# Expert routing: 136 candidate sums per token, and the second expert tile of six heads as three rounded passes

## The reference, cut to what matters

```python
q = (hb @ w_pq).reshape(TOK_BLOCK, PEER_HEADS, 2, PEER_DHALF)
s = jnp.einsum('thpd,hpnd->thpn', q, sub_keys).astype(jnp.float32)
s1, i1 = lax.top_k(s[:, :, 0], PEER_TOPK)          # PEER_TOPK = 16, of 128 keys
s2, i2 = lax.top_k(s[:, :, 1], PEER_TOPK)
cand_s = (s1[..., :, None] + s2[..., None, :]).reshape(..., PEER_TOPK * PEER_TOPK)
top_s, pos = lax.top_k(cand_s, PEER_TOPK)
gate = jax.nn.softmax(top_s, axis=-1)
act = jax.nn.gelu(jnp.einsum('thkd,td->thk', expert_u[idx], hb), approximate=False)
```

## Time and profile before

| | us |
|---|---|
| time, median of 3 runs | 2181.74 |
| lowest and highest | 2181.66, 2182.7 |
| profiled execution, its own time | 2179.3 |
| its span | 2177.5 |

### The profile page before, as it was taken

The page is one execution under the profiler, slowest core; times in us unless marked ns, Lnnn a source line. Parts: engine busy times, 40 slices in busy tenths (PEclk is TensorE's granted clock), DMA queues, the critical chain, the costliest instruction groups (busy, mean ns, idle before and its releaser), DMA issues.

```text
span 2177.5 us, 42049 instructions
## 1 busy us (share of the span) xinstructions
PE 2141.2 (98%) x15321; PEld 1926.4 (88%) x15321; DVE 1460.8 (67%) x2770; ACT 1039.6 (48%) x1757; POOL 104.1 (5%) x78
## 2 busy tenths in 40 slices
PE   9999999999999999999999999999999999999999
PEld 7999998899899987899998668889889999999998
DVE  5556998655655547655685578989886666666665
ACT  4335776533533337433562455458534444444443
POOL 0000000000010000000000004600000000000000
PEclk9999999999999999999999999999999999999999
DMA  6555664455566544555541024344667666655553
GB/s 218 188 182 176 211 191 139 155 193 176 171 209 213 185 137 127 181 176 188 168 145 52 20 98 146 135 159 155 208 224 240 209 204 203 211 185 183 191 185 133
DMA packets 107725, 374.12 MB, mean 172 GB/s; under 512 B 11984, under 2 KB 17888, under 8 KB 107376
## 3 DMA queue, kind: packets, MB, share of 16 engines
q1 hardware_dynamic: 102848, 354.88, 48.8%
q0 software_dynamic: 4784, 18.00, 2.8%
HBM read 362.29 MB, written 13.69 MB: 173 GB/s over the span
## 4 chain that ended last, share of the span: by engine, by line
PE 90%; DVE 6%; ACT 1%; DVEq 1%; issue 1%; DMA 0%; POOL 0%; ACTq 0%
PE bank L357 72%; PE bank L386 5%; PE bank L1590 2%; PE bank L2653 2%; DVE w_lo L309 1%; PE bank L563 1%; PE bank L339 1%; PE bank L341 0%; DVE arena L2839 0%; DVE arena L2832 0%; ACT w_hi L304 0%; PE bank L581 0%; PE bank L2172 0%; DVE arena L2833 0%; PE bank L346 0%
## 5 line engine op out<-in xcount | busy, mean ns | idle before, releaser
L309 DVE TENSOR_TENSOR w_lo<-ring,w_hi 128x1024 fp32r<-128x1024 f32 x575 | 695.4, 1223 | 410.3 <-ACT w_hi L304 408.0
L304 ACT ACTIVATE w_hi<-ring 128x1024 fp32r<-128x1024 f32 x599 | 624.7, 1056 | 627.0 <-PE bank L357 562.8
L357 PE MATMUL bank<-u_hi,w_hi 128*128 128x256 f32 x2712 | 771.4, 284 | 6.6 <-POOL w_lo L309 4.7
L357 PE MATMUL bank<-u_hi,w_lo 128*128 128x256 f32 x2712 | 767.4, 283 | 0.0
L357 PE MATMUL bank<-u_lo,w_hi 128*128 128x256 f32 x2712 | 767.3, 283 | 0.0
L357 PEld LDWEIGHTS bank<-u_hi,w_hi 128*128 128x128 f32 x2712 | 519.7, 192 | 18.8 <-issue 7.4
L357 PEld LDWEIGHTS bank<-u_lo,w_hi 128*128 128x128 f32 x2712 | 519.7, 192 | 7.5 <-issue 0.5
L357 PEld LDWEIGHTS bank<-u_hi,w_lo 128*128 128x128 f32 x2712 | 519.7, 192 | 0.0
L357 PE MATMUL bank<-w_hi,x_hi 128*128 128x512 f32 x992 | 390.7, 394 | 1.3 <-DVE x_lo L2156 0.9
L357 PE MATMUL bank<-w_lo,x_hi 128*128 128x512 f32 x992 | 388.2, 391 | 0.0
L357 PE MATMUL bank<-w_hi,x_lo 128*128 128x512 f32 x992 | 386.1, 389 | 0.0
(11 more groups left out here) (316 smaller groups left out, 1816.9 us busy)
## 6 DMA issues: line engine op xcount, KB each, us to landing
ring<-in_w SPq DMA_DIRECT2D x264, 512.0 KB, 3.6
ring<-in_expert_u SPq DMA_DIRECT2D x128, 512.0 KB, 3.5
ring<-in_expert_v SPq DMA_DIRECT2D x128, 512.0 KB, 4.2
ring<-in_ssm_in SPq DMA_DIRECT2D x40, 512.0 KB, 4.5
gate_dram<-con SPq DMA_DIRECT2D x16, 576.0 KB, 2.8
arena<-gate_dram POOLq DMA_DIRECT2D x9, 1024.0 KB, 8.8
ring<-in_ssm_out SPq DMA_DIRECT2D x16, 512.0 KB, 4.0
ring<-in_w_o SPq DMA_DIRECT2D x16, 512.0 KB, 3.8
```

The lines of the kernel that those rows point to most:

```text
L304: act.activation(w_hi[slot][:, :], ring[slot][:, :], ACT.Copy).then_inc(hi_made[slot], 1)
L309: dve.tensor_tensor(w_lo[slot][:, :], ring[slot][:, :], w_hi[slot][:, :].bitcast(F32), ALU.subtract).then_inc(freed[slot], 1)
L357: mm = pe.matmul(out, left[a], right[b], start=start and n == 0, stop=stop and n == 2, skip_group_check=True)
```

## The change

The candidates become 136: the sums of row 0 with all 16 columns, and of rows 1 to 15 with columns 0 to 7. (A pair that has at least 16 better or equal pairs ahead of it can't be among the 16 best; with both lists in order, no pair of a row past the first with a column past the eighth can.) The row and the column of a pick come from its index by a shift and three small float operations. The second expert tile of heads 1 to 6 goes by `project_split`: ACT makes its `w_hi` at the end of `tiles`, and POOL its `w_lo` right behind that of the first tile. Those of heads 0 and 7 stay with `project`.

```diff
-    "pre_plain": (PH, [0, 0, 0, 1]),
+    "pre_plain": (1, [0, 0, 0, 1]),
+    "pre_second": (PH - 2, [0, 0, 0, 1]),
+    "pre_end": (1, [0, 0, 0, 1]),
...
-            def plain_tile(i):
-                arrived(pe, 3, "pre_plain", i)
+            def second_tile(i):
+                out = bank[(2 * i + 1) % 4][:, 0:T]
                 pe.wait_ge(S("pre_gelu"), 2 * i + 2)
-                project(pe, bank[(2 * i + 1) % 4][:, 0:T], 3).then_inc(freed[3], 1)
+                if 0 < i < PH - 1:
+                    project_split(pe, out, 3, "pre_second", i - 1)
+                else:
+                    arrived(pe, 3, "pre_end" if i else "pre_plain")
+                    project(pe, out, 3).then_inc(freed[3], 1)
...
                 pre(2 * i)
-                multiplied(act, 3, "pre_plain", i)
+                if 0 < i < PH - 1:
+                    split_done(act, 3, "pre_second", i - 1)
+                else:
+                    multiplied(act, 3, "pre_end" if i else "pre_plain")
                 pre(2 * i + 1)
+                if i < PH - 2:
+                    make_hi(act, 3, "pre_second", i)
...
                 if 0 < i < PH - 1:
                     make_lo(pool, 2, "pre_split", i)
+                    make_lo(pool, 3, "pre_second", i - 1)
                 if 0 < i < PH - 2:
                     pool.wait_ge(S("cands_made"), i + 1)
                     make_lo(pool, 0, "route_a", i - 1)
...
-                ins = dve.tensor_tensor(cand.rearrange("p t (a b) -> p t a b", a=TOPK), top[:, 0:TT, :].unsqueeze(3).broadcast_to([P, TT, TOPK, TOPK]),
-                                        top[:, TT:2 * TT, :].unsqueeze(2).broadcast_to([P, TT, TOPK, TOPK]), ALU.add)
+                dve.tensor_tensor(cand[:, :, 0:TOPK], top[:, TT:2 * TT, :],
+                                  top[:, 0:TT, 0:1].broadcast_to([P, TT, TOPK]), ALU.add)
+                ins = dve.tensor_tensor(cand[:, :, TOPK:NCAND].rearrange("p t (a b) -> p t a b", b=NEAR),
+                                        top[:, 0:TT, 1:TOPK].unsqueeze(3).broadcast_to([P, TT, TOPK - 1, NEAR]),
+                                        top[:, TT:2 * TT, 0:NEAR].unsqueeze(2).broadcast_to([P, TT, TOPK - 1, NEAR]), ALU.add)
...
-                dve.tensor_scalar(as_int(flat(best_a)), as_int(flat(best_i)), 4, None, ALU.logical_shift_right)
-                dve.tensor_scalar(as_int(flat(best_b)), as_int(flat(best_i)), 15, None, ALU.bitwise_and)
-                dve.drain()
-                dve.tensor_copy(best_abf, as_int(best_ab))
+                dve.tensor_scalar(as_int(flat(best_row)), as_int(flat(best_i)), 3, None, ALU.logical_shift_right)
+                dve.drain()
+                dve.tensor_copy(best_foundf, as_int(best_found))
+                dve.drain()
+                dve.scalar_tensor_tensor(flat(best_row), flat(best_rowf), 2.0, flat(best_rowf), ALU.is_ge, ALU.mult)
+                dve.tensor_scalar(flat(best_af), flat(best_rowf), 1.0, 0.0, ALU.subtract, ALU.max)
+                dve.drain()
+                dve.scalar_tensor_tensor(flat(best_bf), flat(best_row), -float(NEAR), flat(best_if), ALU.mult, ALU.add)
                 dve.drain()
```

More of the change, by code:

```diff
@@ L195 @@
 FIRST_CONSTS = 4 * P
-SPLIT_RINGS = SPLIT_STAGES + ("mla", "route_a", "route_b", "pre_split", "peer_v", "peer_b") + OUT_RINGS
+SPLIT_RINGS = SPLIT_STAGES + ("mla", "route_a", "route_b", "pre_split", "pre_second", "peer_v", "peer_b") + OUT_RINGS
 RING_OF = {"ssm": ("ssm", "ssm_out"), "attn": ("attn", "attn_out"), "mla": ("mla", "mla_heads"), "mix": ("mix_out",),
-           "peer": ("route_plain", "route_third", "route_a", "route_b", "pre_split", "pre_last", "pre_plain", "gate_u", "peer_v", "peer_b")}
+           "peer": ("route_plain", "route_third", "route_a", "route_b", "pre_split", "pre_last", "pre_plain", "pre_second", "pre_end", "gate_u", "peer_v", "peer_b")}
 LEAD = {**{f"ffn{k}": [(0, f"ffn{k}"), (1, f"ffn{k}"), (2, f"ffn{k}")] for k in range(4)},
@@ L2482, in program @@
         top, top_i, top_f = (area(7680 + 64 * n, 4, TOPK) for n in range(3))
-        cand, cand2 = (area(8192 + 512 * n, TT, TOPK * TOPK) for n in range(2))
-        best, best_i, best_a, best_b, best_af, best_bf, gate = (area(9216 + 32 * n, TT, TOPK) for n in range(7))
-        best_ab, best_abf = area(9280, 2 * TT * TOPK), area(9344, 2 * TT * TOPK)
+        NEAR = TOPK // 2
+        NCAND = TOPK + (TOPK - 1) * NEAR
+        cand, cand2 = (area(8192 + 512 * n, TT, NCAND) for n in range(2))
+        best, best_i, best_row, best_if, best_rowf, best_af, best_bf, gate = (area(9216 + 32 * n, TT, TOPK) for n in range(8))
+        best_found, best_foundf, best_abf = (area(at, 2 * TT * TOPK) for at in (9248, 9312, 9376))
         gate_sum = area(9472, 2, TT)
@@ L2502, in pre @@
                 for n in range(2):
-                    load(sp, 2 + n, io["expert_u"][bass.ds(2 * i + n, 1), :, :], ("pre_split", "pre_plain")[n], i)
+                    load(sp, 2 + n, io["expert_u"][bass.ds(2 * i + n, 1), :, :], ("pre_split", "pre_second")[n], i - n)
             def under_gates(g):
@@ L2521, in peer_sync @@
             queries(0)
-            pre(0)
+            load(sp, 2, io["expert_u"][0:1, :, :], "pre_split", 0)
+            load(sp, 3, io["expert_u"][1:2, :, :], "pre_plain", 0)
             sp.wait_ge(S("h_updated"), 4 * upd["peer"] + 1)
@@ L2533, in peer_sync @@
             load(sp, 2, io["expert_u"][2 * PH - 2:2 * PH - 1, :, :], "pre_last")
-            load(sp, 3, io["expert_u"][2 * PH - 1:2 * PH, :, :], "pre_plain", PH - 1)
+            load(sp, 3, io["expert_u"][2 * PH - 1:2 * PH, :, :], "pre_end")
             under_gates(0)
@@ L2617, in peer_tensor @@
             scores(1)
-            plain_tile(0)
+            second_tile(0)
             for i in range(2, PH):
@@ L2622, in peer_tensor @@
                 scores(i)
-                plain_tile(i - 1)
+                second_tile(i - 1)
             split_tile(PH - 1)
-            plain_tile(PH - 1)
+            second_tile(PH - 1)
             for g in range(AT_CHOICE):
```

## The result

The changed kernel takes 2186.45 us (median of 17 runs, 2184.3 to 2188.46), the one before 2182.7 in the same comparison (17 runs, 2181.36 to 2185.0). The ratio is 1.0017 with a 95% interval of 1.0010 to 1.0024: 3.7 us slower (2.2 to 5.2), so certainly no gain. The forecast was +4.1 (2185.8 on the median then known).

What follows compares the result with a forecast made beforehand. DVE was taken to set routing's period, PE bounding elsewhere. Head 1 +0.28 and heads 2 to 5 +4.36 (1.09 each) gave +4.64, less 0.5 for PE's tile: +4.1, 2185.8 us on the median; range 2180.0 to 2188.2.

Steps and rivals of the forecast that it cites:

- the caught cast: In routing, DVE's cast at 6.50 us waits for POOL's new remainder, which ends at 8.39: +1.75 us per head.
- the rival that was given 0.35: Two-input DVE instructions are held too, so the difference waits for POOL's pair: period about 15.4, 2186.4 us; chance 0.35.
- DVE sets the period: In routing, DVE leads the loop through POOL to PE, 14.17 us per head before; PE needs 12.4 and waits.
- The gains and the price of the arithmetic: On DVE per head: search gains 1.27 us, sums 0.17, index arithmetic loses 0.54; net -0.90, period 13.27 if nothing else moved.
- What is caught at the second place: In routing, DVE's shift comes before POOL's pair of remainders ends at 14.26 and waits: +0.25 us, period 15.27.
- The sum: Over routing: head 1 +0.28 us, heads 2 to 5 +4.36, so +4.64; PE's tile -0.5; transposes +4.1.
- Head 6: In DVE's count for routing, head 6 has no pair of remainders on POOL and adds +0.84 us.
- The transposes wait for DVE: A sign of being wrong, after routing's last head; expected was DVE done at 1441.2, ahead of PE at 1441.8.
- PE's clock: In routing, PE's clock stood at 1.00 with PE busy 91.7 of 100 us, so its longer waits got no price.
- The rival that the cast is not caught: In routing, the cast passes but POOL's work holds the shift: period about 14.3, 2182.0 us, no change; chance 0.13.

Runs made afterwards that it cites:

- e3_cast_later: The changed kernel with DVE's cast of the key indices moved behind the sums and the reciprocal; ratio to the kernel before 1.0018 (1.0009 to 1.0027).
- e5_behind_wait: The changed kernel with POOL's added remainder moved behind its wait for the softmax product; ratio to the kernel before 1.0026 (1.0016 to 1.0036).
- e4_halves: The changed kernel with POOL's added remainder made by two instructions of 512 columns; ratio to the kernel before 1.0021 (1.0012 to 1.0030).

## Why the prediction was right, point by point

The time lies in the range, and the main term, the caught cast, was right. The forecast's mechanism was right only up to there: in the pair of query remainders the rival that was given 0.35 came true, and not the forecast with its 0.40. That the forecast's +4.1 fits the 3.7 of the runs doesn't speak for it, since the rival's +4.7 lies in the same interval (2.2 to 5.2); it is luck that the two were so close in price.

- **DVE sets the period.** Right. In the changed kernel the comparisons lie 15.4 apart in heads 2 to 5 (15.7 once), and PE waits for POOL 1.27 to 3.06 us. I had about 3 in every head. PE needs 15.40 - 2.77 = 12.6 of a head at full clock and not 12.4; nothing hung on it.
- **The gains and the price of the arithmetic.** Right: difference to comparison 1425.88 - 1424.63 = 1.25 in head 6, as worked out; the search 1377.80 - 1374.67 = 3.13 for 3.10; the two sums start 0.10 and 0.32 apart from what follows; head 7, where nothing collides, is 13.28 for 13.27.
- **The cast is caught.** Right: 1.91 us, the sums 8.33 behind the comparison for 8.36.
- **What is caught at the second place.** The step failed in its mechanism, and little in size. I had the shift held, +0.25, and the hold of two-input instructions as a rival, with 0.23 against 0.19 for it and "little" against it. The Trainium skill, page "SBUF — State Buffer", section "Who interferes with whom", has it right in both halves, and 2.36 us for a difference of 32 elements in head 1, 1.89 for a sum in `e3_cast_later` show it. The period is 15.36 to 15.41 for 15.27 (the rival had about 15.4), and 15.72 in head 4.
- **The sum.** Up to PE's last split tile I had +4.64; it was +5.40 (1416.68 - 1315.48 = 101.20 against 1409.00 - 1313.20 = 95.80). Head 1 gave +0.62 for +0.28, since there both instructions are held, one after the other; heads 2 to 5 gave 61.86 - 57.07 = +4.79 for +4.36. Behind it PE won back 0.66 for 0.5. At the transposes +4.74 for +4.1, and in the runs 3.7 (2.2 to 5.2).
- **Head 6.** Missed: 15.40 for 15.02. There is no pair there, but DVE stood 0.43 for no visible reason ahead of its search; some 0.35 more than in their neighbours, in part of that kind, also stood in one of heads 2 to 5, in head 3 before and in head 4 after.
- **The transposes wait for DVE.** The prediction named this as a sign of being wrong, with DVE at 1441.2 and PE at 1441.8. It came, by some 0.2 us: PE's last four products start at 1443.70, 0.216 apart, the last at 1444.35, so the first transpose was due at 1444.57; it came at 1444.75, just behind DVE's last reduction (1443.46 + 1.21 = 1444.67). The pause in head 6 brought DVE there. Before, DVE ended 1.07 ahead.

```profile
1443.46 1.21 DVE L2866 TENSOR_REDUCE arena<-arena 128x64 f32<-128x1024 f32 x1
```

```profile
1443.70 1.03 PE L388 MATMUL bank<-u_t,ring 128*128 128x256 f32 x4
1444.75 0.87 PE L2640 MATMUL bank<-con,arena 128*128 128x128 f32 x6
```

- **PE's clock.** Wrong. I put no price on it because it had stood at 1.00 in a stretch of 100 us with PE at 92%; but a mean over 100 us says nothing of waits of 3 us (below). In this execution the slow products lay where PE had time to spare.
- **The rival that the cast is not caught** I priced at no change. `e5_behind_wait` is that case, and it is not at no change but at 1.0026 (1.0016 to 1.0036), with 15.88 a head: I had let POOL run its four remainders without a gap from the weighing on, although whoever keeps POOL out of the cast's way also starts it later.

## What to carry to other kernels

Before work is given to an idle GpSimd, list what VectorE does with casts, shifts or two SBUF inputs in each stretch that GpSimd would be busy; in a chain led by VectorE the moved instruction costs what is left of it when VectorE arrives, however small the instruction that waits. Here cutting it up or moving it between waits only moved that cost. VectorE's single-input searches and reductions were not held: beside POOL's pair of 1373.55 to 1378.30 one FIND_INDEX8 took 0.29 and the long reduction 1.21, as they did in head 6 with POOL idle. So what helps is a stretch of these, or a place where VectorE has slack. And a part that seems to gain on its own (136 sums, -1.7 us) can be hidden by one that costs more: time the parts singly.

## What the runs showed of the hardware that I had not expected

*Behind most waits of 2 to 3 us PE's granted clock was halved, and the products ran at half speed for some 3 us.* In the changed kernel, the timeline of PE behind a wait of 3.06 us:

```profile
1401.29 0.55 PE L359 MATMUL bank<-u_hi,w_hi 128*128 128x256 f32 x1 [3.06 <-POOL w_lo L311]
1401.63 0.41 PE L359 MATMUL bank<-u_lo,w_hi 128*128 128x256 f32 x1
1401.85 0.41 PE L359 MATMUL bank<-u_hi,w_lo 128*128 128x256 f32 x1
...
1404.37 0.28 PE L359 MATMUL bank<-u_hi,w_lo 128*128 128x256 f32 x1
1404.49 0.28 PE L359 MATMUL bank<-u_hi,w_hi 128*128 128x256 f32 x1
```

and the granted clock in that stretch (busy time by stretch; the clock is the third number from the end):

```profile
1401.00:1404.00 3.00, 2.71 (x13) 2.75 (x14) 2.93 (x9) 0.00 (x0) 2.48 (x2) 0.50 0.44 164
```

The products start 0.21 apart and not 0.12: 1.2 GHz instead of 2.4. The same followed the wait of 2.77 at 1370.21; behind waits of 1.59, 1.27 and 1.44 (1354.81, 1385.60 and 1416.68) the clock stayed. In the changed kernel this cost nothing, as PE had time to spare there: the 24 products took 4.3 to 4.4 us for 2.94, and the next wait was shorter by as much. In `e3_cast_later` it came after the last wait:

```profile
1418.50 0.55 PE L359 MATMUL bank<-u_hi,w_hi 128*128 128x256 f32 x1 [2.74 <-POOL w_lo L311]
...
1422.81 1.05 PE L2581 MATMUL bank<-arena 128*128 128x128 f32 x8
```

The tile took 4.31 us for the 2.94 of the changed kernel (1416.68 to 1419.62), and the transposes came 1.05 later than there although the periods are the same. In `e5_behind_wait` the last tile took 4.44, behind a wait of 2.01; the clock was 0.67 from 1418 to 1421.

The length of the wait alone doesn't settle it. The same execution of `e3_cast_later` has three waits of the same length, and behind the first the clock stayed at 1.00 and the 24 products took 2.94, while behind the second they took 4.44:

```profile
1372.08 0.35 PE L359 MATMUL bank<-u_hi,w_hi 128*128 128x256 f32 x1 [2.74 <-POOL w_lo L311]
...
1387.47 0.55 PE L359 MATMUL bank<-u_hi,w_hi 128*128 128x256 f32 x1 [2.75 <-POOL w_lo L311]
```

Over the five profiles with periods above 15, the 24 products took 4.2 to 4.5 us behind twelve waits, of 1.96 to 3.28 us, and 2.9 to 3.0 behind that one and behind the twelve of 1.23 to 1.81. What decides between them no run here shows. The profiled executions whose period is above 15 show a mean clock of 0.997, the others 0.998 or 0.999; over all runs the two groups meet at 0.998. The Trainium skill, page "TensorE: Matmul & The Clock Gate", section "Part 1: The HAM clock gate", names the same two levels, 1.2 and 2.4 GHz, and the trace agrees.

*A held instruction of DVE gets in between two instructions of POOL that follow on each other without a gap.* Seen in head 1 of the changed kernel, in `e4_halves` and in `e5_behind_wait`: each of DVE's instructions passes where one of POOL's ends, and the next of DVE's waits for the whole next one of POOL's. Left open is what the waits of 0.2 and 0.4 us on DVE are, which stand in one head or another of every kernel here.
